# A decoder layer's expert gathers: the ring of 14 parts split into two circles of seven

## The chip, the cores and the metric

One core of a Trainium2 chip runs the whole layer in one launch. The metric is the device time of that core in microseconds (us), median over runs.

## What is computed

One decoder layer on 512 tokens of width 1024, in float32. A mixing sub-layer (stick-breaking attention with 8 heads and a gated MLP, side by side) comes first, then the PEER sub-layer, then a gated per-layer embedding; each ends in a LayerNorm over `alpha*x + f(x)`. The change lies in the PEER sub-layer. For every token and each of 8 heads, product keys choose 16 of 16384 experts. An expert is a row `u` and a row `v` of 1024 floats each:

```python
def block(args):                      # 128 tokens
    xb, idb, gb = args
    ue = jnp.take(u_tab, idb, axis=0)
    h = jnp.einsum('thkd,td->thk', ue, xb)
    act = gb * jax.nn.gelu(h, approximate=False)
    ve = jnp.take(v_tab, idb, axis=0)
    return jnp.einsum('thk,thkd->td', act, ve)
```

So 512 * 8 * 16 pairs of rows, 8 KB each, 537 MB, are fetched from HBM by index.

## The kernel before

The 512 tokens are four tiles of 128, one token to a partition. A *unit* is one tile with one head; 32 units stand in a fixed order (`UNITS`), and each has 16 *rows*. Row n = 16u + c is one expert for each of the 128 tokens: one indirect DMA, issued by POOL (GpSimd) at L691, takes 128 descriptors of 8 KB from the table `uv`, which holds each expert's u and v one behind the other. Its destination is 2 of the 14 parts of `ring` (L283), a part being 1024 floats on every partition: u in the first part, v in the next.

What happens to a row, engine by engine:

- POOL's `gather_unit` (L697) waits until the two parts are free and issues the gather, in the order of n.
- DVE's `dots` (L1906) waits for the landing and multiplies u with the token's vector and sums (L1914), which counts `dots_done` up; u is then no longer needed.
- ACT's `activate_rows` (L1521) takes two rows at a time: Gelu of the sums (L1526), times the gate (L1529), and the v part scaled in place by it (L1536).
- PE's `combine` (L1256) adds the scaled v part to the unit's sum in PSUM by eight transposing matmuls (L1269) and counts `slot_free` up; v is then no longer needed.

DVE ranks the next unit's keys between dots, and all of DVE, ACT and PE also do the mixing sub-layer of later tiles and the end of earlier ones between the rows, at steps written out by hand (`background`, one step for every two rows). SP loads weights by plain DMAs, which run on the same 16 DMA engines.

The ring's arithmetic: row n has its u at part `(8 + 11n) % 14` and its v in the part after it. Row n+5's v then falls on row n's u, and row n+9's u on row n's v. So `U_LIFE` is 5 and `V_LIFE` is 9: before the gather of row n, POOL waits for `slot_free` of row n-9 (L713), and then for `dots_done` of row n-5 (L718). Where a row's u falls on the last part its v falls on part 0, and it is *torn*: two gathers of 4 KB descriptors (L716 and L720). The first goes out ahead of the wait for `dots_done`.

```python
if torn(n):
    gather(u_row(u, c), u, c, 0, rows_in[c % LANDINGS])
if n >= U_LIFE and not (u == NU - 1 and c >= HOMED):
    pool.wait_ge(dots_done, n - U_LIFE + 1)
```

Eight landing semaphores (`LANDINGS`) go round with n. Of the last unit, rows from `HOMED` (13) on have homes of their own outside the ring, rows from `LATE` (11) on come with their v cut in half or left out, and seven small gathers fetch the rest at the end (L728 to L731). In the first unit the ring still holds weights of the first tile: the output projection's (parts 0 to 7), later scratch (8 and 9), the gating projection's (10 to 12, free in two steps, `gv_halves`), and a LayerNorm gain (13).

Of the kernel before, what the change touches and what calls it, by code (L numbers as in the profile page):

```python
# [24 lines left out]
PH, TOPK, NKEY = 8, 16, 128  # L25
# [6 lines left out]
MASKED = -float(2 ** 30)  # L32
SEED = 1597463007.0

U_LIFE, V_LIFE = 5, 9
PARTS = U_LIFE + V_LIFE
PART_STEP = 11
assert PART_STEP * U_LIFE % PARTS == PARTS - 1
FIRST_PART = 8
LANDINGS = 8  # L40
GRP = 2
OUT_PIECES = ((0, 512), (512, 832), (832, 1024))
# [6 lines left out]
HOMED = TOPK - 3  # L49
# [11 lines left out]
NU = len(UNITS)  # L61
# [17 lines left out]
assert RUN_END[NR - 1 - RUN_TILE[::-1].index(1)] == 21 and RUN_END[NR - 1 - RUN_TILE[::-1].index(2)] == 26  # L79


def part_of(n):

    return (FIRST_PART + PART_STEP * n) % PARTS


def torn(n):

    return n < (NU - 1) * TOPK + HOMED and part_of(n) == PARTS - 1


def landed(n):

    return sum(32 if torn(m) else 16 for m in range(n % LANDINGS, n + 1, LANDINGS))
# [124 lines left out]
def build(nc, a, out):  # L219
    ctx = ExitStack()  # L220
    with ctx:
# [3 lines left out]
        def sem(name):  # L225
            return ctx.enter_context(nc.semaphore(name))
# [71 lines left out]
        def row_home(u, c):  # L298
            return (v_flat, wq_a, wq_r)[c - HOMED]

        def u_row(u, c):

            if u == NU - 1 and c >= HOMED:
                return row_home(u, c)[:, 0:D]
            part = part_of(u * TOPK + c)
            return ring[:, part * D:(part + 1) * D]

        def v_row(u, c):

            if u == NU - 1 and c >= HOMED:  # L310
                return row_home(u, c)[:, D:2 * D]
            part = (part_of(u * TOPK + c) + 1) % PARTS
            return ring[:, part * D:(part + 1) * D]

        def whole_row(u, c):

            if u == NU - 1 and c >= HOMED:
                return row_home(u, c)
            part = part_of(u * TOPK + c)
            return ring[:, part * D:(part + 2) * D]  # L320

        late_sum = v_row(NU - 1, LATE)[:, HALF:D]
        y_1 = u_row(NU - 1, LATE)[:, 0:HALF]


# [165 lines left out]
        dots_done = sem("dots_done")  # L491
# [171 lines left out]
        @block.gpsimd  # L663
        def _(pool):
            nc.gpsimd.memset(ident[:, :], 0.0).then_inc(const_ready, 1)
            nc.gpsimd.memset(neg_tri[:, :], -1.0).then_inc(const_ready, 1)
            nc.gpsimd.memset(neg_one[:, :], -1.0).then_inc(const_ready, 1)
            nc.gpsimd.memset(neg_mask[:, :], MASKED).then_inc(const_ready, 1)
            nc.gpsimd.memset(ones[:, :], 1.0).then_inc(const_ready, 1)
            nc.gpsimd.iota(iota16[:, :], pattern=[[1, TOPK]], base=0, channel_multiplier=0,  # L670
                           allow_small_or_imprecise_dtypes=True).then_inc(const_ready, 1)
            pool.wait_ge(const_ready, 6)
            nc.gpsimd.affine_select(out=ident[:, :], in_=ident[:, :], compare_op=ALU.not_equal, fill=1.0,
                                    base=0, pattern=[[-1, P]], channel_multiplier=1).then_inc(const_ready, 1)
            nc.gpsimd.affine_select(out=neg_tri[:, :], in_=neg_tri[:, :], compare_op=ALU.is_ge, fill=0.0,
                                    base=0, pattern=[[-1, P]], channel_multiplier=1).then_inc(const_ready, 1)
            nc.gpsimd.affine_select(out=neg_mask[:, :], in_=neg_mask[:, :], compare_op=ALU.is_ge, fill=0.0,
                                    base=0, pattern=[[-1, P]], channel_multiplier=1).then_inc(const_ready, 1)
            pool.wait_ge(ws_in, 16)
            nc.gpsimd.affine_select(out=wsT, in_=wsT, compare_op=ALU.is_ge, fill=0.0, base=0,  # L680
                                    pattern=[[0, G], [1, P]], channel_multiplier=-1).then_inc(ws_masked, 1)


            for buf, ready, done in ((l_0, l_ready, l_masked), (e_0, a_ready, a_masked)):
                pool.wait_ge(ready, 1)
                blk = buf.rearrange("p i (h n) -> p (i h) n", n=P)
                nc.gpsimd.affine_select(out=blk, in_=blk, compare_op=ALU.is_gt, fill=0.0, base=0,
                                        pattern=[[0, AH], [1, P]], channel_multiplier=-1).then_inc(done, 1)

            def gather(dst, u, c, first, signal):  # L690
                nc.gpsimd.indirect_dma_start(  # L691
                    out=dst, out_offset=None, in_=a["uv"][:, :],
                    in_offset=bass.IndirectOffsetOnAxis(ap=ids[:, u % 4, c:c + 1], axis=0),
                    element_offset=first,
                ).then_inc(signal, 16)

            def gather_unit(u):  # L697
                if u:
                    pool.wait_ge(ids_ready, u + 3)
                for c in range(TOPK):  # L700
                    n = u * TOPK + c
                    if u == 0 and c in (0, 1, TOPK // 2):
                        pool.wait_ge(ids_ready, (0, 1, TOPK // 2).index(c) + 1)
                    if u == 0 and c == 0:
                        pool.wait_ge(score_done, 1)
                    if u == 0 and c == 4:
                        pool.wait_ge(gv_halves, 1)
                    if u == 0 and c == 8:
                        pool.wait_ge(gv_halves, 2)
                    if u == NU - 1 and c >= HOMED:  # L710
                        pool.wait_ge(q_done, NU)
                    elif n >= V_LIFE:
                        pool.wait_ge(slot_free, n - V_LIFE + 1)  # L713
                    end = PART if u == NU - 1 and c >= LATE else 2 * D
# [5 lines that stand above are left out]
                        gather(v_row(u, c)[:, 0:end - D], u, c, D, rows_in[c % LANDINGS])  # L720
                    elif u == NU - 1 and c >= TOPK - 2:
                        gather(u_row(u, c), u, c, 0, rows_in[c % LANDINGS])
                    else:
                        gather(whole_row(u, c)[:, 0:end], u, c, 0, rows_in[c % LANDINGS])

            for u in range(NU):
                gather_unit(u)
            for c in range(TOPK - 2, TOPK):  # L728
                gather(v_row(NU - 1, c)[:, 0:HALF], NU - 1, c, D, values_in[c - TOPK + 2])
            for c in range(LATE, TOPK):  # L730
                gather(v_row(NU - 1, c)[:, HALF:D], NU - 1, c, PART, late_in[c - LATE])  # L731
# [1493 lines left out]
```

## Time and profile before

| | us |
|---|---|
| median of 3 runs | 1422.82 (1420.91 to 1423.07) |
| the profiled execution | 1421.98 |
| its span, first to last instruction | 1420.3 |
| PE busy / DVE / ACT / POOL | 1130.9 / 1078.1 / 938.8 / 625.0 |
| POOL's gathers, 556 instructions | 619.9 |
| DVE's dots, 512 instructions | 623.1 (467.7 and 155.4) |

The profile is of one execution. "Busy" is the time in which an engine ran an instruction; waiting, branching and issuing by SP are not counted. A DMA share is the mean busy share of 16 DMA engines; packets that overlap on an engine can bring it above 1. The granted TensorE clock was 0.896 of full speed over the span.

### The profile page before, as it was taken

Reading aid. Unit: us, or ns where it says so; the run is one execution under the profiler, and the core shown is the slowest. Engines: PE = TensorE matmul, PEld = TensorE weight load, DVE = VectorE, ACT = ScalarE, POOL = GpSimd, SP = SyncE. Lnnn points to the kernel's source line nnn. Section 1 sums busy time; section 2 is a strip of 40 time slices with the busy share of each in tenths; the row PEclk is TensorE's granted clock in tenths of the full one; section 3 lists DMA queues with packets and bytes.
Section 4 is the critical chain, followed back from the end, with each engine's and each line's share of the span. In section 5 each row is a group of like instructions: output and inputs, shape, how many; then the busy total and the mean of one; then the engine's idle time right before and its main releaser. Section 6 shows DMA issues by size and latency. Waiting matters only on the chain.

```text
span 1420.3 us, 19525 instructions
## 1 busy us (share of the span) xinstructions
PE 1130.9 (80%) x6884; PEld 890.8 (63%) x6884; DVE 1078.1 (76%) x2602; ACT 938.8 (66%) x1617; POOL 625.0 (44%) x572
## 2 busy tenths in 40 slices
PE   9999999998789877696756987877667866776566
PEld 4567777676677776666656566765555655555455
DVE  1488877778778887678766668988887788878857
ACT  2245778679877988766645666667666766667563
POOL 1044444344444554444433434444444555444451
PEclk9999999999889999998777988898789988888968
DMA  9899999999999999999999999999999999999994
GB/s 351 311 383 409 422 425 425 426 425 425 402 426 419 424 423 425 425 424 417 431 422 425 426 426 406 426 425 426 426 426 413 404 423 426 426 425 426 425 400 170
DMA packets 94476, 581.98 MB, mean 410 GB/s; under 512 B 10237, under 2 KB 15781, under 8 KB 31914
## 3 DMA queue, kind: packets, MB, share of 16 engines
q0 software_dynamic: 79552, 536.91, 90.5%
q1 hardware_dynamic: 14826, 43.83, 8.0%
q8 instruction: 54, 0.88, 0.2%
q14 instruction: 44, 0.36, 0.1%
HBM read 578.60 MB, written 2.10 MB: 409 GB/s over the span
## 4 chain that ended last, share of the span: by engine, by line
DMA 40%; PE 30%; DVE 15%; ACT 8%; issue 6%; POOL 2%; SPq 0%; DVEq 0%; POOLq 0%; ACTq 0%
DMA arena<-in_uv,ids 39%; PE ps L1269 11%; DVE arena L1914 8%; ACT arena L1536 3%; PE ps L1082 3%; PE ps L948 3%; POOL arena L691 2%; PE ps L1159 2%; PE ps L740 2%; ACT actv L1529 1%; PE ps L757 1%; PE ps L896 1%; PE ps L824 1%; PE ps L821 1%; ACT L1576 1%
## 5 line engine op out<-in xcount | busy, mean ns | idle before, releaser
L691 POOL DMA_INDIRECT arena<-in_uv,ids x556 | 619.9, 1115 | 734.5 <-DVE hid L1914 338.0
L1269 PE MATMUL ps<-ident,arena 128*128 128x128 f32 x4076 | 608.9, 308 | 273.0 <-ACT arena L1536 271.2
L1269 PEld LDWEIGHTS ps<-ident,arena 128*128 128x128 f32 x4076 | 533.3, 159 | 364.6 <-ACT arena L1536 321.4
L1914 DVE CUSTOM_DVE_ANT_1 arena<-arena 128x1024 f32<-128x1024 f32 x384 | 467.7, 1224 | 187.2 <-DMA arena<-in_uv,ids 183.8
L1536 ACT ACTIVATE arena<-arena,actv 128x1024 f32<-128x1024 f32 x511 | 554.2, 1131 | 0.3 <-ACT actv L1529 0.2
L1526 ACT ACTIVATE gel<-hid 128x2 f32<-128x2 f32 (+1 forms) x257 | 52.0, 202 | 356.0 <-DVE hid L1914 353.2
L1914 DVE CUSTOM_DVE_ANT_0 arena<-arena 128x1024 f32<-128x1024 f32 x128 | 155.4, 1223 | 61.1 <-DMA arena<-in_uv,ids 58.5
L1529 ACT ACTIVATE actv<-gel,gates 128x1 f32<-128x1 f32 x511 | 122.9, 287 | 8.4
L948 PE MATMUL ps<-arena 128*128 128x128 f32 x992 | 120.3, 281 | 0.0
L948 PEld LDWEIGHTS ps<-arena 128*128 128x128 f32 x992 | 118.2, 199 | 0.0
L1082 PE MATMUL ps<-arena 128*128 128x384 f32 x192 | 65.9, 486 | 0.0
L1159 PE MATMUL ps<-arena 128*128 128x512 f32 (+2 forms) x160 | 60.2, 524 | 0.0
L1576 ACT ACT_TABLE_LOAD x45 | 57.7, 1283 | 0.8
L1584 ACT ACT_TABLE_LOAD x45 | 57.7, 1283 | 0.8
L1082 PEld LDWEIGHTS ps<-arena 128*128 128x128 f32 x192 | 34.6, 190 | 19.1
L896 PE MATMUL ps<-arena 128*128 128x512 f32 x96 | 43.9, 600 | 0.7 <-DVE arena L1924 0.4
L1159 PEld LDWEIGHTS ps<-arena 128*128 128x128 f32 x160 | 29.9, 201 | 20.9 <-issue 18.5
L1914 DVE DVE_READ_ACCUMULATOR2_ANT hid<- 128x1 f32 x512 | 41.9, 82 | 0.0
L747 PE MATMUL ps<-arena 128*128 128x512 f32 x64 | 29.4, 599 | 1.3 <-ACT arena L1427 0.7
L896 PEld LDWEIGHTS ps<-arena 128*128 128x128 f32 x96 | 17.7, 194 | 18.9 <-issue 17.5
L740 PE MATMUL ps<-arena 128*128 128x512 f32 x64 | 28.9, 594 | 0.0
L1783 DVE TENSOR_TENSOR cands<-cands,topf 128x512 f32<-128x512 f32 x31 | 21.4, 691 | 1.1
(269 smaller groups left out, 1018.1 us busy)
## 6 DMA issues: line engine op xcount, KB each, us to landing
arena<-in_wq SPq DMA_DIRECT2D x9, 1024.0 KB, 10.2
arena<-in_uv,ids POOLq DMA_INDIRECT x556, 3.8
arena<-in_w_out SPq DMA_DIRECT2D x2, 2048.0 KB, 11.3
arena<-in_w_gate SPq DMA_DIRECT2D x1, 4096.0 KB, 17.2
arena<-in_w_out SPq DMA_DIRECT2D x3, 1024.0 KB, 13.1
arena<-in_w_k SPq DMA_DIRECT2D x4, 512.0 KB, 7.9
arena<-in_w_q SPq DMA_DIRECT2D x2, 1024.0 KB, 10.2
arena<-in_w_v SPq DMA_DIRECT2D x2, 1024.0 KB, 10.2
```

What stands on the lines that cost most here:

```text
L691: nc.gpsimd.indirect_dma_start(out=dst, out_offset=None, in_=a["uv"][:, :], in_offset=bass.IndirectOffsetOnAxis(ap=ids[:, u % 4, c:c + 1], ...
L740: i = mm(ps[:, bank, :], xt(k), w[:, k * AW:(k + 1) * AW], start=(k == 0), stop=(k == KD - 1), skip_group_check=True)
L896: i = mm(ps[:, bank, :], src[:, c, :], w[:, c, j * HALF:(j + 1) * HALF], start=(c == 0), stop=(c == WB - 1))
L948: i = mm(ps[:, 7, half * P:(half + 1) * P], wq[b][k][:, half * P:(half + 1) * P], x1T[t][:, k, :], start=(k == 0), stop=(k == KD - 1))
L1082: i = mm(ps[:, piece_bank(p), 0:REST], w[:, b * D + k * P:b * D + (k + 1) * P], xT[:, k, :], start=(k == 0), stop=(k == KD - 1), skip_grou ...
L1159: m = mm(ps[:, bank, place:place + c1 - c0], acc[t][:, k * P:(k + 1) * P], w_gate[:, k, c0:c1], start=(k == 0 and place == 0), stop=(k == ...
L1269: i = mm(ps[:, run_bank(r) + k // 4, (k % 4) * P:(k % 4 + 1) * P], v_row(u, c)[:, k * P:(k + 1) * P], ident[:, :], is_transpose=True, star ...
L1529: fn(actv[:, i, c:c + 1], gel[:, i, c:c + 1], ACT.Copy, scale=gates[:, i, c:c + 1])\
L1536: fn(r, r, ACT.Copy, scale=actv[:, i, c:c + 1]).then_inc(scaled, 1)
L1576: act.preload_act_table_set("natural_log_exp_and_others")
L1584: act.preload_act_table_set("gelu_and_others")
L1914: v.tensor_tensor_reduce(out=r, in0=r, in1=x1[t], scale=1.0, scalar=0.0, op0=ALU.mult, op1=ALU.add, accum_out=hid[:, i, c:c + 1]).then_inc ...
```

## The change

The 14 parts become two circles of seven, one for rows of even n and one for odd n. In its circle a row's u is at `(first + 2 * (n // 2)) % 7` and its v in the next part of that circle. Row n+6's v then falls on row n's u, and row n+8's u on row n's v: `U_LIFE` is 6 and `V_LIFE` 8. A row whose u falls on the last part of its circle is torn, one row in seven. Two waits of the first unit move (from row 4 to 5 and from row 8 to 7), and the last unit's homed rows wait for `dots_done` of row n-8, the one that used their landing semaphore before.

```diff
--- before.py
+++ after.py
@@ -32,11 +32,12 @@
 MASKED = -float(2 ** 30)
 SEED = 1597463007.0
 
-U_LIFE, V_LIFE = 5, 9
+U_LIFE, V_LIFE = 6, 8
 PARTS = U_LIFE + V_LIFE
-PART_STEP = 11
-assert PART_STEP * U_LIFE % PARTS == PARTS - 1
-FIRST_PART = 8
+CIRCLE = PARTS // 2
+PART_STEP = 2
+assert PART_STEP * U_LIFE // 2 % CIRCLE == CIRCLE - 1
+FIRST_PART = (0, 6)
 LANDINGS = 8
 GRP = 2
 OUT_PIECES = ((0, 512), (512, 832), (832, 1024))
@@ -79,14 +80,24 @@
 assert RUN_END[NR - 1 - RUN_TILE[::-1].index(1)] == 21 and RUN_END[NR - 1 - RUN_TILE[::-1].index(2)] == 26
 
 
-def part_of(n):
-
-    return (FIRST_PART + PART_STEP * n) % PARTS
+def place_of(n):
+
+    return (FIRST_PART[n % 2] + PART_STEP * (n // 2)) % CIRCLE
+
+
+def u_part(n):
+
+    return n % 2 * CIRCLE + place_of(n)
+
+
+def v_part(n):
+
+    return n % 2 * CIRCLE + (place_of(n) + 1) % CIRCLE
 
 
 def torn(n):
 
-    return n < (NU - 1) * TOPK + HOMED and part_of(n) == PARTS - 1
+    return n < (NU - 1) * TOPK + HOMED and place_of(n) == CIRCLE - 1
 
 
 def landed(n):
@@ -302,21 +313,21 @@
 
             if u == NU - 1 and c >= HOMED:
                 return row_home(u, c)[:, 0:D]
-            part = part_of(u * TOPK + c)
+            part = u_part(u * TOPK + c)
             return ring[:, part * D:(part + 1) * D]
 
         def v_row(u, c):
 
             if u == NU - 1 and c >= HOMED:
                 return row_home(u, c)[:, D:2 * D]
-            part = (part_of(u * TOPK + c) + 1) % PARTS
+            part = v_part(u * TOPK + c)
             return ring[:, part * D:(part + 1) * D]
 
         def whole_row(u, c):
 
             if u == NU - 1 and c >= HOMED:
                 return row_home(u, c)
-            part = part_of(u * TOPK + c)
+            part = u_part(u * TOPK + c)
             return ring[:, part * D:(part + 2) * D]
 
         late_sum = v_row(NU - 1, LATE)[:, HALF:D]
@@ -703,12 +714,13 @@
                         pool.wait_ge(ids_ready, (0, 1, TOPK // 2).index(c) + 1)
                     if u == 0 and c == 0:
                         pool.wait_ge(score_done, 1)
-                    if u == 0 and c == 4:
+                    if u == 0 and c == 5:
                         pool.wait_ge(gv_halves, 1)
-                    if u == 0 and c == 8:
+                    if u == 0 and c == 7:
                         pool.wait_ge(gv_halves, 2)
                     if u == NU - 1 and c >= HOMED:
                         pool.wait_ge(q_done, NU)
+                        pool.wait_ge(dots_done, n - LANDINGS + 1)
                     elif n >= V_LIFE:
                         pool.wait_ge(slot_free, n - V_LIFE + 1)
                     end = PART if u == NU - 1 and c >= LATE else 2 * D
```

## Rows read from the trace of the kernel before

**Rows 1.** The page: busy times, DMA share in 40 slices, the gathers' queue, their issues.
```profile
PE 1130.9 (80%) x6884; PEld 890.8 (63%) x6884; DVE 1078.1 (76%) x2602; ACT 938.8 (66%) x1617; POOL 625.0 (44%) x572
...
DMA  9899999999999999999999999999999999999994
...
q0 software_dynamic: 79552, 536.91, 90.5%
...
arena<-in_uv,ids POOLq DMA_INDIRECT x556, 3.8
```

**Rows 2.** Stretches: length, busy PE, PEld, DVE, ACT, POOL (count), clock, DMA share, GB/s.
```profile
160.00:180.00 20.00, 20.00 (x133) 15.65 (x128) 14.67 (x38) 12.51 (x22) 7.25 (x8) 1.00 1.02 426
...
340.00:360.00 20.00, 13.29 (x114) 11.90 (x112) 18.29 (x49) 18.82 (x28) 8.47 (x9) 0.89 0.97 399
...
860.00:880.00 20.00, 15.61 (x116) 14.20 (x115) 17.76 (x28) 14.06 (x27) 9.78 (x8) 0.91 0.96 392
1080.00:1100.00 20.00, 10.41 (x73) 8.83 (x71) 17.45 (x48) 11.27 (x21) 10.52 (x9) 0.91 1.00 404
1100.00:1120.00 20.00, 20.00 (x114) 14.85 (x113) 14.78 (x26) 13.73 (x26) 10.08 (x8) 0.92 0.98 387
1200.00:1220.00 20.00, 10.88 (x67) 9.31 (x66) 17.17 (x48) 11.50 (x21) 10.62 (x9) 0.81 1.01 425
1340.00:1360.00 20.00, 13.82 (x66) 10.11 (x65) 16.68 (x38) 14.02 (x24) 10.54 (x8) 0.77 0.95 385
```

**Rows 3.** Order of time: start, length, what, idle before and releaser; POOL's holes.
```profile
356.23 1.16 POOL L691 DMA_INDIRECT arena<-in_uv,ids  x1 [5.79 <-issue]
...
1348.58 1.22 DVE L1914 CUSTOM_DVE_ANT_1 arena<-arena 128x1024 f32<-128x1024 f32 x1
...
1353.14 2.01 POOL L691 DMA_INDIRECT arena<-in_uv,ids  x1 [4.64 <-issue]
```

**Rows 4.** Order of time near the end of the gathers, the same columns.
```profile
1373.11 1.23 DVE L1914 CUSTOM_DVE_ANT_1 arena<-arena 128x1024 f32<-128x1024 f32 x1 [1.21 <-DMA arena<-in_uv,ids]
...
1373.75 3.67 PE L1269 MATMUL ps<-ident,arena 128*128 128x128 f32 x16 [1.75 <-ACT arena L1536]
...
1375.54 1.23 DVE L1914 CUSTOM_DVE_ANT_1 arena<-arena 128x1024 f32<-128x1024 f32 x1 [1.20 <-DMA arena<-in_uv,ids]
...
1377.56 0.94 POOL L691 DMA_INDIRECT arena<-in_uv,ids  x1 [1.15 <-PE ps L1269]
...
1381.59 0.94 POOL L691 DMA_INDIRECT arena<-in_uv,ids  x1 [0.30 <-issue]
...
1386.63 1.23 DVE L1914 CUSTOM_DVE_ANT_1 arena<-arena 128x1024 f32<-128x1024 f32 x1 [0.61 <-DMA arena<-in_uv,ids]
```

**Rows 5.** Waits of POOL: us in total, times, longest.
```profile
POOL arena L691 <- DVE hid L1914: 338.0, 186, 6.4
POOL arena L691 <- PE ps L1269: 271.2, 158, 5.4
```

**Rows 6.** DMA queues (packets, MB, share) in 704:718 (two), 1200:1300 and 5:30 us.
```profile
q1 hardware_dynamic: 113, 3.64, 60.2%
q0 software_dynamic: 331, 2.36, 40.1%
...
q0 software_dynamic: 6265, 42.48, 101.0%
...
q1 hardware_dynamic: 5999, 9.33, 103.0%
```

**Rows 7.** Order of time: gathers and combines early on, while PE is full.
```profile
170.40 0.98 POOL L691 DMA_INDIRECT arena<-in_uv,ids  x1 [3.37 <-PE ps L1269]
...
446.23 1.03 POOL L691 DMA_INDIRECT arena<-in_uv,ids  x1 [0.30 <-issue]
...
447.32 1.91 PE L1269 MATMUL ps<-ident,arena 128*128 128x128 f32 x16
```

**Rows 8.** Order of time: row 4's gather in the first unit.
```profile
82.33 0.93 POOL L691 DMA_INDIRECT arena<-in_uv,ids  x1 [1.55 <-PE ps L747]
```

## Prediction

> **What bounds the kernel now.** I read the page first. The gathers' queue holds 90.5% of all 16 DMA engines' time, the DMA digit is 9 in every slice but the second and the last, and PE, the busiest engine, is busy for 80% [rows 1]. So bytes on the move set the pace. The table of stretches sharpens it: where nothing disturbs the stream it moves 425 or 426 GB/s at a DMA share of 1.01 or 1.02, whether PE is busy 20 us of 20 or 11 [rows 2]. A row is 1.05 MB, so it takes 2.47 us there. A change to the ring can then act in three ways only: it fills stretches that lie below that rate, it opens new ones, or it makes the same bytes dearer.
>
> Second, the stretches below it. 340 to 360, 860 to 880, 1100 to 1120 and 1340 to 1360 us stand at shares of 0.97, 0.96, 0.98 and 0.95, with 385 to 399 GB/s [rows 2]. The order of time on POOL has a hole in each of them, and one more between: five gathers before which POOL sat idle for about 5 us, the first at 356.23 and the last at 1353.14 [rows 3]. The last can be followed. Counted back from the last dot product, the one of row 492 ended at 1349.80 (1348.58 and 1.22) and freed the u part for row 497's gather; that gather started 3.34 us later [rows 3]. At row 508 the same step, from the end of row 503's dot (1375.54 and 1.23) to the gather at 1377.56, took 0.79 [rows 4]. So five times POOL itself is some 2.55 us late after its wait is over. What holds it there the trace doesn't tell.
>
> Third, which wait holds a gather. The view of waits gives DVE's dot 338.0 us and PE's combine 271.2 [rows 5], but it names the semaphore that moved last, not the count that was needed. In order of time, row 508's gather came 0.79 us after the dot of row 503, while the combine that it needs, of row 499, was over before PE began rows 500 and 501 at 1373.75 [rows 4]. Followed through the trace like this, the dot of row n-5 comes after the combine of row n-9 for all but some 17 rows: the u part's life is the gate, the v part's has slack. From that gather to its own dot at 1386.63 lie 9 us [rows 4]: four rows are in flight.
>
> **The change, part by part.** The sum is made against the profiled execution's own time, 1421.98 us (span 1420.3), 0.8 below the median of the runs.
>
> *One row more ahead on the u side, one fewer on the v side.* Row n's gather now waits for the dot of n-6 and the combine of n-8. At row 508 that is the dot of 502, over at 1374.34, and the combine of 500, the first eight of the sixteen matmuls that began at 1373.75 and took 3.67, so about 1375.6 [rows 4]. PE becomes the later of the two, and the release moves from 1376.77 to 1375.6: 1.2 us earlier, not the full 2.47 that it would be behind a quick combine. In an undisturbed stretch this is worth nothing, since the DMA engines have work for 9 us anyway. In the holes it covers a gather that is 2.55 us late. What they cost now: against a share of 1.01 the four stretches lack 0.04, 0.05, 0.03 and 0.06 of 20 us, 0.8 + 1.0 + 0.6 + 1.2 = 3.6 us; by bytes against 425 GB/s they lack 1.2 + 1.6 + 1.8 + 1.9 = 6.5 us [rows 2]. I take 3.6, since the share counts idle engines alone while smaller packets lower GB/s too, and I take all of it back, since 1.2 us of cover is more than a hole loses on the mean. The ends are 0 and 6.5.
>
> *A torn row in every seven.* Counted by the two formulas, 73 rows are torn where 37 were: 36 more gathers, 592 for 556. Each makes 128 packets of 8 KB into 256 of 4 KB and adds 16 small ones of its own, 144 packets. What a packet costs beside its bytes comes from two stretches: 444 packets with 6.00 MB took 100.3% of 16 engines for 14 us, 224.7 us, and 6265 with 42.48 MB took 101.0% for 100 us, 1616 us [rows 6]. Solved, a packet costs 8.1 ns and a MB 36.9 us. 144 packets on 16 engines are 0.073 us a row, 2.6 us for 36. The upper end comes from a stretch of small packets, 5999 with 9.33 MB at 103.0% for 25 us, 412 us [rows 6]: with the same 1616 us that is 12.4 ns and 4.0 us. The lower end is 0: shares over 1 say that packets overlap, and the overhead may be what overlaps. I take 2.6, from a stretch of the big packets that the stream is made of. POOL issues 36 times more, at 0.94 and a gap of 0.30 as at 1381.59 [rows 4], 45 us in all. It is busy 44% [rows 1] and waits for the ring before nearly every gather, so that hides; uncovered, a torn row would leave 1.24 us later. The first gather of a torn row goes before the wait for the dot, which only deepens the queue.
>
> *PE as the gate early on.* At 160 to 180 us PE is busy 20 us of 20 [rows 2], and combines run late there: a gather at 170.40 already had POOL idle for 3.37 us behind one [rows 7]. The dearest place that I find is at 446.23. That gather (row 142) would now wait for the first half of the sixteen matmuls of 447.32, until some 448.3, and start near 449.1, 2.9 us later than it did [rows 7]. A gather needs 3.8 us from issue to landing (that median is of the quarter-sized ones at the end [rows 1]) and a whole row some 1.8 more, so 454.7. Row 141 landed at about 452.1, ahead of its dot, and the stream wants the next 2.47 later, at 454.6: it just misses. I take 0.4 for all such places, with ends of 0 and 3.5 (four such places, each short by 0.9, what a gather's issue can grow by: it took 0.94 at best and 2.01 at 1353.14 [rows 3]).
>
> *Start and end, at nothing.* The waits for the projections of the gate move from rows 4 and 8 to rows 5 and 7. Gathers run there already and the third slice (71 to 106 us) is at 9 [rows 1], so the stream is full; without that cover it would be the 1.55 us that POOL waited for PE at 82.33 [rows 8]. The three homed rows get a wait for the dot of row n-8: for row 511 that is row 503's, over at 1376.77, while its gather came at 1381.59 behind others that POOL issues one after another [rows 4]. Only POOL's last seven gathers stand behind it, and none is held.
>
> The sum: -3.6 + 2.6 + 0.4 = -0.6, and the time 1421.4 us.
>
> **The rivals.** *Faster: the holes cost what the bytes say.* Then 6.5 come back: -6.5 + 2.6 + 0.4 = -3.5, 1418.5. For it: 385 GB/s is 9% below the rate where the share is 6% below, and the holes lie in the low stretches. Against it: 1080 to 1100 is low as well, 404 GB/s, and has no hole [rows 2].
>
> *Slower: PE's combine gates the stream.* With v parts kept for eight rows, a gather can't leave before PE is done with row n-8. It decides where a combine ends over some 14 us after its row landed: seven rows of 2.47 in flight, less the 3.8 that a gather needs [rows 1]. If it stands at the holes too, nothing comes back there, and the near misses cost their end: 2.6 + 3.5 = 6.1, 1428.1. For it: PE full in the first 300 us. Against it: at row 508 the combine still releases earlier than the dot did.
>
> *The longer life does nothing.* If POOL's delay starts anew at whatever row it waits for and eats the cover, the holes stay and the packets are paid: +2.6 + 0.4, 1425.0.
>
> *Every added gather holds up the stream for its fixed time.* If the queue ran dry for the 3.8 us from issue to landing [rows 1], 36 would cost 137 us, 1559. Against it: 100 us move 42.48 MB, forty rows, with some 9 us of flight each [rows 6, 4], so these times overlap. The Trainium skill (DMA: Bandwidth & Descriptors, Anatomy of one DMA) speaks against splitting: some 2.0 us fixed for each such DMA, beside its bytes at 436 GB/s; paid one after another that would be an estimated 72 us for 36. The 37 torn rows of the kernel before show no gap of that kind.
>
> **How the numbers follow.** 0.2% of this kernel, 2.8 us, is about what a measurement can tell from no change: faster is below 1420.0, slower above 1425.7. The forecast has 0.51. The faster rival has 0.26, and with it the case that the packets cost nothing, 1418.8 with the forecast's other terms. PE as the gate has 0.16, the useless longer life 0.06 (a third of it over the line, with packets at their upper end), the fixed time 0.01. So faster 0.26, same 0.55, slower 0.19. The range runs from 1417.5, past the faster cases, to 1426.5, past the useless life and into PE's gate.
>
> **What would show it.** Right: 592 gathers; the stretches around POOL's late gathers at a share of 1.01; packets under 8 KB in the middle of the span nearly doubled and its rate 1 GB/s lower; POOL's waits shifted from the dot to the combine. Wrong: new stretches below 1.00 before 460 us with PE full (PE's gate), holes as deep as now (the useless life), or an unchanged rate with the stream over 3 us earlier (free packets, or dearer holes).

## The result and the profile after

The changed kernel takes 1424.12 us, median of 22 runs (1421.4 to 1428.38), beside 1422.71 for 22 runs of the kernel before (1419.86 to 1424.46). The ratio is 1.0013 (1.0007 to 1.0019): 1.8 us slower, between 1.0 and 2.7; by the medians alone 1.4. The forecast was 1421.4, 0.6 us faster than the profiled execution of before. The time lies inside the range given and within the 0.2% called no change, but the sign is the other one. The profiled execution took 1423.77 us (span 1422.1, granted clock 0.903 of full speed).

The page of the changed kernel, the lines that answer to [rows 1], with the group of POOL's gathers from its fifth part:

```profile
PE 1126.8 (79%) x6884; PEld 881.7 (62%) x6884; DVE 1080.1 (76%) x2602; ACT 939.0 (66%) x1617; POOL 678.2 (48%) x608
...
DMA  9899999999999999999999999999999999999993
...
q0 software_dynamic: 84800, 536.91, 90.5%
...
L702 POOL DMA_INDIRECT arena<-in_uv,ids x592 | 673.2, 1137 | 681.0 <-PE ps L1281 393.4
...
arena<-in_uv,ids POOLq DMA_INDIRECT x592, 11.4
```

592 gathers, as counted. POOL's largest wait is for PE, and a gather now takes a median of 11.4 us from issue to landing. (The 3.8 of the kernel before covers only the few gathers of which every landing mark was recorded; the same ring in v8_late, below, shows 9.9.) (Lines 702, 1281 and 1926 of the changed kernel are 691, 1269 and 1914 of the kernel before.) The view of waits of the changed kernel, POOL's two largest, beside [rows 5]:

```profile
POOL arena L702 <- PE ps L1281: 393.4, 212, 5.6
POOL arena L702 <- DVE hid L1926: 147.2, 66, 6.4
```

The dot's share fell from 338.0 to 147.2 us and the combine's rose from 271.2 to 393.4: the gate moved to PE, as forecast. Followed row by row, the combine of row n-8 comes after the dot of row n-6 for 336 of the 500 rows from 9 to 508. The table of stretches of the changed kernel (columns as in [rows 2]):

```profile
160.00:180.00 20.00, 20.00 (x125) 15.55 (x124) 14.21 (x36) 11.94 (x22) 8.51 (x8) 1.00 1.00 392
340.00:360.00 20.00, 13.32 (x120) 12.20 (x119) 18.09 (x51) 19.09 (x28) 11.74 (x11) 0.94 1.01 419
440.00:460.00 20.00, 17.95 (x127) 14.65 (x126) 17.62 (x37) 19.72 (x31) 9.91 (x8) 1.00 0.93 369
860.00:880.00 20.00, 16.71 (x104) 14.57 (x103) 18.63 (x38) 14.29 (x25) 7.95 (x8) 0.74 1.01 426
1100.00:1120.00 20.00, 18.73 (x108) 14.53 (x109) 15.73 (x32) 14.61 (x27) 8.96 (x10) 0.91 1.01 426
1200.00:1220.00 20.00, 10.56 (x64) 8.98 (x64) 17.24 (x43) 11.52 (x23) 10.33 (x10) 0.83 1.02 425
...
1260.00:1280.00 20.00, 17.16 (x87) 11.91 (x87) 15.54 (x32) 14.28 (x27) 10.35 (x9) 0.91 1.00 399
...
1340.00:1360.00 20.00, 12.84 (x69) 10.24 (x70) 17.70 (x43) 14.38 (x25) 10.55 (x10) 0.84 1.02 426
```

The four low stretches of before, at 0.95 to 0.98 and 385 to 399 GB/s [rows 2], stand at 1.01 or 1.02. New low ones came: 160 to 180 us (392 GB/s where [rows 2] has 426), 440 to 460 (369), and 1260 to 1280 (399), around a gather that POOL, itself late, issued at 1277.86; its row and the two behind it still landed 2.45 to 2.48 us apart, on time. One stretch of the kernel before, not shown until now:

```profile
440.00:460.00 20.00, 19.70 (x135) 15.76 (x135) 17.47 (x35) 19.71 (x31) 10.36 (x10) 1.00 1.01 418
```

So the changed kernel gains where the holes were and loses early on. POOL's late gathers themselves now come at other rows (99, 191, 283, 375 and 467), so that the four stretches are full doesn't yet show that the longer life covers a late gather; a_u5 below bears on that. The order of time of the changed kernel shows the first of the new places on POOL and PE, then the gather of row 142 that the prediction picked, then the last dot (columns as in [rows 3]):

```profile
160.92 1.92 POOL L702 DMA_INDIRECT arena<-in_uv,ids  x1 [3.12 <-PE ps L1281]
...
164.93 3.60 PE L752 MATMUL ps<-arena 128*128 128x512 f32 x8
168.37 1.04 PE L1281 MATMUL ps<-ident,arena 128*128 128x128 f32 x8
...
169.68 0.94 POOL L702 DMA_INDIRECT arena<-in_uv,ids  x1 [3.37 <-PE ps L1281]
...
174.45 0.98 POOL L702 DMA_INDIRECT arena<-in_uv,ids  x1 [2.52 <-PE ps L1281]
...
178.78 0.94 POOL L702 DMA_INDIRECT arena<-in_uv,ids  x1 [2.11 <-PE ps L1281]
...
447.77 1.91 PE L1281 MATMUL ps<-ident,arena 128*128 128x128 f32 x16
...
449.08 1.85 POOL L702 DMA_INDIRECT arena<-in_uv,ids  x1 [4.97 <-PE ps L1281]
...
1392.61 1.23 DVE L1926 CUSTOM_DVE_ANT_1 arena<-arena 128x1024 f32<-128x1024 f32 x1
```

At 169.68 goes row 36's gather. It waited 3.37 us for the combine of row 28, the eight matmuls at 168.37; PE had a v projection of 3.60 us (L752) ahead of them. It landed at 175.81, 2.44 behind row 35 and so on time, 6.1 us after its issue. Row 37, issued next, landed 2.93 behind it, and row 38, whose gather at 174.45 had waited again, 3.44 behind that, where 2.47 keep the stream full: some 1.5 us lost in three rows.

### The profile page after: what moved, and what is told of

It reads as the page before. It is cut to its first block, busy times and chain, and to the rows that moved or that the text cites. A ratio compares the mean times of both kernels' runs of the same rounds, so it can differ in the third digit from the quotient of the medians.

```text
span 1422.1 us, 19535 instructions
## 1 busy us (share of the span) xinstructions
PE 1126.8 (79%) x6884; PEld 881.7 (62%) x6884; DVE 1080.1 (76%) x2602; ACT 939.0 (66%) x1617; POOL 678.2 (48%) x608
## 4 chain that ended last, share of the span: by engine, by line
DMA 40%; PE 30%; DVE 12%; ACT 8%; issue 6%; POOL 4%; SPq 0%; POOLq 0%; DVEq 0%; ACTq 0%
DMA arena<-in_uv,ids 39%; PE ps L1281 11%; DVE arena L1926 7%; ACT arena L1548 4%; POOL arena L702 4%; PE ps L1094 3%; PE ps L960 3%; PE ps L1171 2%; PE ps L759 2%; ACT actv L1541 1%; PE ps L769 1%; PE ps L752 1%; ACT L1596 1%; ACT L1588 1%; PE ps L833 1%
## 5 line engine op out<-in xcount | busy, mean ns | idle before, releaser
L702 POOL DMA_INDIRECT arena<-in_uv,ids x592 | 673.2, 1137 | 681.0 <-PE ps L1281 393.4
L1281 PEld LDWEIGHTS ps<-ident,arena 128*128 128x128 f32 x4076 | 527.5, 158 | 372.6 <-ACT arena L1548 330.8
L1588 ACT ACT_TABLE_LOAD x45 | 57.7, 1283 | 0.8
L1596 ACT ACT_TABLE_LOAD x45 | 57.7, 1283 | 0.8
L752 PE MATMUL ps<-arena 128*128 128x512 f32 x64 | 28.9, 594 | 0.0
## 6 DMA issues: line engine op xcount, KB each, us to landing
arena<-in_uv,ids POOLq DMA_INDIRECT x592, 11.4
```

The costliest lines, as they stand in the source:

```text
L702: nc.gpsimd.indirect_dma_start(out=dst, out_offset=None, in_=a["uv"][:, :], in_offset=bass.IndirectOffsetOnAxis(ap=ids[:, u % 4, c:c + 1], ...
L1281: i = mm(ps[:, run_bank(r) + k // 4, (k % 4) * P:(k % 4 + 1) * P], v_row(u, c)[:, k * P:(k + 1) * P], ident[:, :], is_transpose=True, star ...
L1588: act.preload_act_table_set("natural_log_exp_and_others")
L1596: act.preload_act_table_set("gelu_and_others")
```

## The experiments

Every kernel is compared with 29 to 35 runs of the kernel before on the same chip (median 1421.47 for v8_only, a_u5 and the two split kernels, 1421.8 for the three light kernels and shift3, 1421.58 for the rest); differences in us come from the ratio, and the interval behind a ratio is at 95%. "v8" below means the wait for the combine of row n-8 where the kernel before waits for that of n-9, and nothing else.

**The combine's wait alone** (v8_only): the old ring, the wait one row tighter.

```diff
-                    elif n >= V_LIFE:
-                        pool.wait_ge(slot_free, n - V_LIFE + 1)
+                    elif n >= V_LIFE - 1:
+                        pool.wait_ge(slot_free, n - V_LIFE + 2)
```

> The kernel before, where the gather of row n also waits for the combine of row n-8 (it needs only n-9). So the new gate of the change alone: no longer life for u, no more torn rows. Theory A: +1 to +3 us, from new short gaps of the stream at 165 to 180 us and 445 to 460 us, where PE is full, and holes unchanged. Rival B (all of the change's loss beyond the holes is this gate): +5 to +6 us. If the gate is harmless: 0.

1425.27 us (1421.25 to 1431.32, 12 runs), ratio 1.0029 (1.0014 to 1.0043): +4.1 us, between 2.0 and 6.1. Its stretches show the same two places:

```profile
160.00:180.00 20.00, 20.00 (x122) 15.33 (x121) 13.63 (x34) 11.83 (x22) 8.05 (x8) 1.00 0.99 400
440.00:460.00 20.00, 19.80 (x128) 15.03 (x127) 17.49 (x37) 19.72 (x32) 10.54 (x9) 1.00 0.99 387
```

The shorter v life alone costs more than the whole change does, and ten times the 0.4 that I took for it.

**Where it costs** (v8_early, v8_late): the same wait for rows under 200 only, and from 200 on only.

```diff
-                    elif n >= V_LIFE:
-                        pool.wait_ge(slot_free, n - V_LIFE + 1)
+                    elif n >= V_LIFE - 1:
+                        pool.wait_ge(slot_free, n - V_LIFE + 1 + (n < 200))
```

(v8_late has `n >= 200` and leaves the `elif` as it was.)

> The kernel before, where the gathers of rows 8 to 199 also wait for the combine of row n-8, and the rest for n-9 as before. Theory A (the gate bites while PE does the later tiles' projections and attention between the combines, in the first 550 us): the whole of what the gate cost for all rows, +3 to +4 us. Rival (the gate costs a little at every row): 200/512 of it, +1.6 us.

> The same wait for row n-8, for rows from 200 on alone. Theory A: 0, within 0.1%. Rival: 312/512 of what the gate costs for all rows, +2.5 us.

v8_early: 1424.83 (11 runs), 1.0023 (1.0012 to 1.0035), +3.3 us. v8_late: 1421.95 (12 runs), 1.0000 (0.9992 to 1.0009), nothing that shows. The first stretch, of v8_early and then of v8_late:

```profile
160.00:180.00 20.00, 20.00 (x137) 15.65 (x134) 14.62 (x37) 13.71 (x25) 8.30 (x8) 1.00 1.00 401
```

```profile
160.00:180.00 20.00, 20.00 (x131) 15.65 (x128) 15.05 (x38) 13.17 (x25) 7.56 (x9) 1.00 1.01 425
```

The price lies in the first 200 rows, before some 600 us. In the other 312 no price of the tighter wait shows (-1.1 to 1.3 us).

**One row tighter still** (v7_only): the wait for the combine of n-7, in the old ring.

```diff
-                    elif n >= V_LIFE:
-                        pool.wait_ge(slot_free, n - V_LIFE + 1)
+                    elif n >= V_LIFE - 2:
+                        pool.wait_ge(slot_free, n - V_LIFE + 3)
```

> The kernel before, where every gather also waits for the combine of row n-7: two rows tighter than its ring needs. The dose. In the profile of before a combine ends 7.4 us after its row landed at the median, 10.9 at 90 in 100 and up to 13.9; seven rows less the lead leave some 11 us. Theory A: many rows of the first 550 us and some later ones bind, +10 to +25 us, mostly before 550 us. If the gate's cost doesn't come from late combines: twice the cost of one row, +8 us, evenly spread.

1452.97 (1448.09 to 1463.25, 4 runs), 1.0206 (1.0185 to 1.0228): +29 us, more than the 10 to 25 expected. Two of its stretches, from a profile of the slowest of the four runs:

```profile
160.00:180.00 20.00, 20.00 (x124) 15.47 (x123) 12.38 (x35) 12.49 (x22) 8.00 (x8) 1.00 0.89 336
...
1200.00:1220.00 20.00, 11.71 (x66) 10.25 (x67) 15.79 (x40) 11.06 (x20) 9.74 (x9) 0.70 1.01 425
```

Full rate late, far from it early. The prices for a v life of nine, eight and seven rows are 0, 4 and 29: the lag of the combine has a tail that a life of nine just covers and eight just doesn't.

**Is it PE's load?** (light, light_v8, light_after): three kernels with less work on PE. Half of the contraction is left out of the later tiles' k, q, v and gate projections and of the output projection, so these compute something else; the gathers, dots and combines are all there. `light` does this to the kernel before, `light_v8` to v8_only, `light_after` to the changed kernel.

```diff
-                    i = project_tok(piece_bank(p), w_v, x_cols(b), 4 * half, 4 * half + 4)
+                    for k in range(4 * half, 4 * half + 2):
...
-                    for k in range(4 * half, 4 * half + 4):
+                    for k in range(4 * half, 4 * half + 2):
...
-                for c in range(WB):
+                for c in range(WB // 2):
```

> The kernel before with PE relieved: the projections of the later tiles' k, q, v and gate over half of their depth (four of eight matmuls each half piece becomes two), and the output projection of the later tiles over two of four blocks. It leaves that part of the computation out; bytes, DVE, ACT and POOL are as before. It is the base for the next two. The stream bounds, so both theories expect it within 0.2% of before.

> The same relieved kernel, with every gather also waiting for the combine of row n-8. The gate alone cost +0.29% (0.14 to 0.43) at full PE work. Theory A (the gate costs because PE's other work makes the early combines late): under a third of that against the relieved kernel, 0 to +1.4 us, and the stretches 160:180 and 440:460 at a DMA share of 1.00 or more. Rival (the wait itself costs, whatever PE does, as one more wait of POOL before every gather or later issues all along): +4 us again.

> The changed kernel relieved in the same way. Theory A: with the gate harmless the change shows its gain, 0 to 3 us faster than the relieved kernel before. Rival: +2 us as at full PE work.

light: 1422.01, 1.0003 (0.9994 to 1.0012). light_v8: 1425.46, 1.0026 (1.0014 to 1.0038), which is 3.45 over light. light_after: 1422.86, 1.0002 (0.9989 to 1.0015), level with light. By these counts the relief did not take the price of the wait away. The stretches say where it did and where it didn't. Of light_v8:

```profile
160.00:180.00 20.00, 17.36 (x109) 12.78 (x107) 14.77 (x38) 12.39 (x24) 7.97 (x8) 1.00 1.02 426
440.00:460.00 20.00, 16.16 (x116) 13.45 (x117) 17.32 (x35) 19.45 (x30) 10.15 (x10) 1.00 1.00 410
460.00:560.00 100.00, 78.52 (x607) 71.13 (x606) 79.77 (x195) 85.16 (x136) 49.38 (x43) 0.90 1.01 416
```

and of light:

```profile
440.00:460.00 20.00, 17.71 (x114) 14.05 (x113) 17.59 (x37) 19.72 (x32) 10.58 (x9) 0.83 1.01 424
460.00:560.00 100.00, 79.90 (x624) 72.76 (x623) 81.53 (x200) 86.05 (x139) 50.51 (x44) 0.90 1.01 424
```

At 160 to 180 us, where PE fell from 20.00 busy to 17.36, the stream is back at 426. Between 440 and 560 the relief took little off PE in the long stretch (80.24 in v8_only, 78.52 here), and the rate stays below light's: 410 against 424 and 416 against 424, (14/424)*20 + (8/424)*100 = 2.5 us. The order of time of light_after at the first place (its combine is line 1283):

```profile
170.98 2.13 PE L1283 MATMUL ps<-ident,arena 128*128 128x128 f32 x16 [0.57 <-ACT arena L1550]
```

The combine there waits for ACT, not behind a projection. So early on it is PE's queue that makes the combine late. What makes it late between 440 and 560 us the relief doesn't tell: ACT is busy 19.45 of 20 us there, and the output projection waits for DVE as well; neither was tested.

**The landings.** Each gather leaves sixteen landing marks in the trace, and a row can be used at its last one. How much later the last mark came than in the kernel before (for the two light kernels: than in light), us, median of seven rows, one execution of each, worked out from the marks (some 7% of them are missing in the kernel before, none in the changed one):

```
row   changed  v8_only  v8_early  v8_late  a_u5  |  light_v8  light_after
 31     -0.8     -0.8      1.4      0.5     0.1  |    -1.1       -1.9
 60      2.1      2.2      4.2      0.3     2.1  |    -1.8       -1.8
139      0.4      1.4      4.5     -0.4     1.5  |    -1.1       -1.1
194      3.3      4.0      6.8     -0.4     3.5  |     1.3        1.9
230      1.5      3.4      5.8     -0.7     1.9  |     0.6       -0.3
395      2.2      3.6      5.9     -0.4     3.3  |     1.3        1.2
506      1.7      3.6      5.9      0.8     4.0  |     1.9        1.0
```

Down a column, two steps stand in the changed kernel, v8_only and v8_early alike: 2.8 to 3.0 us between rows 31 and 60, and 2.3 to 2.9 between 139 and 194. v8_late has neither. With PE relieved the first step is gone, the second isn't. In the changed kernel 1.5 of the first is rows 37 and 38 as above; another 1.5 is row 47, whose first mark came on time and whose last one came 3.7 later than a full stream would bring it behind row 46 (in the kernel before, row 48's came 2.2 late); no wait of POOL explains that. What makes the second step stays open.

**The packets** (p1_split36, p2_split255): more torn rows in the old ring, in which any row can be fetched as two gathers. 36 more, and 255 more.

```diff
-    return n < (NU - 1) * TOPK + HOMED and part_of(n) == PARTS - 1
+    return n < (NU - 1) * TOPK + HOMED and (part_of(n) == PARTS - 1 or n % 2 == 0)
```

(p1_split36 has `n % PARTS == 10` in place of `n % 2 == 0`.)

> The kernel before with its own ring (u for 5 rows, v for 9) and 36 more torn rows (every n that leaves 10 by 14), so 73 as in the changed kernel; nothing else. Theory A (packets paid, holes won back, combines as a new gate): 36 times 0.073 us, +2.6 us, up to 4.0; about 1.002 of before. Rival B (packets are free, the whole difference is PE's combine as the gate): 0, within 0.1%. The holes on POOL come once every 105 gathers in both profiles, so they should come every 98 - 6 = 92 rows here and stay holes of the stream.

> The kernel before with every even row of the ring torn as well, 255 more gathers than before. The packets' price enlarged. Theory A: 255 times 0.073 us, +18.6 us (0.05 to 0.111 a row: 13 to 28). Rival B: 0 to 3 us. A third reading, that each added gather costs the stream some fixed time of the order of 1 us, gives over 100 us. POOL then issues 1.57 gathers a row, 1.95 us of 2.47, so it should still keep up; holes on POOL come every 105 gathers, so 8 instead of 5, some 3 more at 0.8 us.

p1_split36: 1421.9 (12 runs), 0.9999 (0.9989 to 1.0009). p2_split255: 1431.71 (6 runs), 1.0064 (1.0051 to 1.0077), +9.1 us, below the 13 to 28 expected. The issues on p2_split255's page, and its gathers' queue in 1200 to 1300 us:

```profile
arena<-in_uv,ids POOLq DMA_INDIRECT x811, 8.8
...
q0 software_dynamic: 9111, 42.08, 101.7%
```

255 splits at 9.1 us are 0.036 us each (0.028 to 0.043), half of the 0.073 that I worked out from two stretches. (The 9.1 holds two more late gathers of POOL as well, seven for five, so 0.036 is if anything too much.) For 36, at the same price each, that is 1.3 us (1.0 to 1.5). p1_split36 alone can't tell 1.3 from nothing, and its added gathers also shift the rows at which POOL is late.

**Shifting POOL's late gathers** (shift3, shift11): three and eleven rows more are torn early on, which moves the late gathers and does hardly anything else.

```diff
-    return n < (NU - 1) * TOPK + HOMED and part_of(n) == PARTS - 1
+    return n < (NU - 1) * TOPK + HOMED and (part_of(n) == PARTS - 1 or n in (10, 24, 38))
```

(shift11 has `n in range(10, 76, 6)`.)

> The kernel before with three more torn rows, 10, 24 and 38, and nothing else. POOL is late once in 105 gathers, so its five holes move three rows forward, to rows 102, 200, 298, 396 and 494, where by the trace of before DVE has just been quick: the next landings lie 8.3 to 8.6 us behind the release, against 6.6 to 8.2 at rows 105 to 497. Theory A (what a hole costs is decided by the row that it falls on; much of the change's gain came from moving the holes, not from the longer life): 2 to 4 us faster than before. Rival (a hole costs the same wherever it falls while u lives five rows): 0.

> The kernel before with eleven more torn rows, every sixth from 10 to 70: POOL's holes move eleven rows forward, to rows 94, 192, 290, 388 and 486, where the next landings lie 8.5 to 11.6 us behind the release by the trace of before. Theory A (a hole costs by where it falls): 1 to 3 us faster than before, like the kernel with three more torn rows, of which the stream's gaps were half of those before. Rival (where they fall doesn't matter): +0.4 us for the packets.

shift3: 1420.97 (11 runs), 0.9993 (0.9984 to 1.0002). shift11: 1421.81 (11 runs), 0.9997 (0.9988 to 1.0005). Neither is clear of no difference; what a shift alone could bring is 1 us or so. The late gathers moved as meant: rows 102, 200, 298, 396 and 494 in shift3, 95, 194, 293, 392 and 491 in shift11. In p1_split36 they stand at rows 99, 191, 283, 374 and 467, none of which lands between 860 and 880 us, and still that stretch of p1_split36 is low:

```profile
860.00:880.00 20.00, 15.75 (x93) 13.43 (x92) 17.57 (x28) 12.93 (x25) 10.06 (x9) 0.74 0.99 390
```

**The longer u life taken back** (a_u5): the changed kernel, whose gather of row n waits for the dot of n-5 again. Two circles, torn rows and the wait for PE stay.

```diff
-                    if n >= U_LIFE and not (u == NU - 1 and c >= HOMED):
-                        pool.wait_ge(dots_done, n - U_LIFE + 1)
+                    if n >= U_LIFE - 1 and not (u == NU - 1 and c >= HOMED):
+                        pool.wait_ge(dots_done, n - U_LIFE + 2)
```

> The changed kernel, where the gather of row n also waits for the dot of row n-5, as before the change (it needs only n-6). So the longer life of u is taken back; packets and PE's gate stay. Theory A: slower than the changed kernel by what the holes cost, 3.6 to 6.5 us, so some +5 to +8 us over before, and gaps of the stream at POOL's late gathers again. If the longer life did nothing: equal to the changed kernel, +1.4 us over before.

1426.28 (1423.05 to 1428.35, 12 runs), 1.0027 (1.0016 to 1.0038), +3.8 us, less than the 5 to 8 expected. The changed kernel's ratio is 0.0014 lower, so the longer life is worth 2.0 us; with both intervals, 0.2 to 3.8. Both are late at the gather of row 375. The stretch there, of a_u5 and then of the changed kernel:

```profile
1040.00:1060.00 20.00, 12.06 (x72) 10.18 (x70) 15.76 (x40) 11.06 (x20) 11.18 (x10) 0.77 0.98 392
```

```profile
1040.00:1060.00 20.00, 13.73 (x74) 11.73 (x72) 15.85 (x42) 11.39 (x23) 11.86 (x10) 0.67 1.02 428
```

The same late gather opens a hole with five rows ahead and none with six. By the marks, rows 375 and 376 of a_u5 land 2.81 and 2.80 us behind the row before and row 467, at the next late gather, 3.17; in the changed kernel these are 2.44, 2.53 and 2.48. The four stretches that were low in the kernel before don't tell the two apart. Of a_u5:

```profile
340.00:360.00 20.00, 14.46 (x118) 13.39 (x116) 16.98 (x52) 17.81 (x28) 11.80 (x10) 0.90 1.01 423
860.00:880.00 20.00, 16.02 (x112) 14.42 (x112) 18.63 (x36) 13.91 (x25) 8.36 (x10) 0.88 1.01 423
1100.00:1120.00 20.00, 18.41 (x116) 13.82 (x115) 15.63 (x33) 14.29 (x25) 11.61 (x10) 0.99 1.02 424
1340.00:1360.00 20.00, 11.69 (x67) 9.00 (x66) 17.43 (x45) 14.02 (x24) 12.08 (x11) 0.84 1.01 425
```

They are full with u kept for five rows as well: the 36 added gathers bring POOL's late ones to other rows.

No kernel here clearly beats both. A ring that keeps u five rows and v nine up to row 200, and six and eight after it, should by these numbers have the gain without the price; it wasn't tried, since the two layouts would have to hand over in the middle of the stream.

## Why the prediction was wrong

**The step that failed is "PE as the gate early on".** It was given 0.4 us, with ends of 0 and 3.5. Alone it measured 4.1 (2.0 to 6.1), 3.3 of it in the first 200 rows and nothing that shows behind them. Two things in the step were wrong. First, I looked for the dearest single gather and named row 142's. In the changed kernel that gather came at 449.08, forecast near 449.1, and its row landed 2.46 us behind row 141: it did not miss at all. (In v8_only and v8_early rows 142 and 143 together lost 1.0 and 0.7 us against v8_late: this place can cost, but it is a part.) The other one in the same group I passed over: [rows 7] shows POOL idle for 3.37 us behind a combine at 170.40, and I did not follow the rows behind it. In the changed kernel one gather after another waits for PE there, the queue runs down, and 1.5 us are lost by row 38. Row 47 and the second step of the table hold the rest, and how they come about no run shows. Second, the lead that a gather needs: I took 3.8 + 1.8 = 5.6 us from issue to landing, the first term from the quarter-sized gathers of the end. Row 36 took 6.1 and row 142 6.4 (449.08 to 455.50), each with the row before it still landing. Of the prediction's own signs of being wrong one came true: a new stretch below 1.00 before 460 us, at 0.93 from 440 on, though its rows landed on time.

**The packets** were right in kind and, if 36 cost by the piece what 255 did, half in size: 1.3 us for the forecast 2.6. That lies between the bounds given; that packets overlap would fit it, but no run shows that this is the reason.

**The holes.** All four stretches came back to a share of 1.01, as forecast, but not by what I forecast: in a_u5, without the longer life, they are as full. The added gathers move POOL's late ones to other rows, which the prediction did not reckon with. Where the late ones now fall, rows 375 and 467 show the cover at work. It is worth 2.0 us (0.2 to 3.8) where 3.6 was forecast. "A hole in each of them" was too simple: 860 to 880 us is low in p1_split36 without one.

**The sum.** Packets and moved holes come together, so I add runs. p1_split36 has both, at -0.1 (-1.6 to 1.3); with 4.1 for the gate that is 4.0, and a_u5, which has the three together, measured 3.8. Less 2.0 for the longer life, 4.0 gives +2.0; measured +1.8 (1.0 to 2.7). Packets and holes, forecast at -3.6 + 2.6 = -1.0, came out at -0.1 - 2.0 = -2.1, within their intervals somewhat better. The gate came out 3.7 worse, and it alone turned the sign.

**The rivals.** "PE's combine gates the stream" had the mechanism that decided and, at its end, nearly the price; its claim that nothing would come back at the holes was wrong, and so was its time, 1428.1. The faster rival took 6.5 for the holes; no run gave back that much. "The longer life does nothing" falls by row 375. The fixed time for each gather falls by p2_split255: 255 more gathers cost 9.1 us, while 255 times the 3.8 us from issue to landing would be 969. The Trainium skill (DMA: Bandwidth & Descriptors, Anatomy of one DMA) puts some 2.0 us of fixed cost on each such DMA, an estimated 510 us for 255; the run shows under 2% of that; here the next gather is in flight all the while, as the 8.8 us from issue to landing on p2_split255's page tell for rows of 2.47.

**Start and end** cost nothing that shows: the landings are within 0.8 us of before at row 31, and the last seven gathers run back to back.

## What to carry to other kernels

When a ring trades a row of life between two consumers, price the shorter life by the tail of that consumer's lag in its busiest stretch, over several rows in a row, not by one gather or by the stage in which the profile looks tight on the mean. A wait can be tightened alone in the old kernel before anything is rebuilt, and for one part of the loop at a time; here one line told the price, and a second its place. A price too small to measure can be multiplied: 255 splits told what 36 couldn't.

## What the runs showed that was not expected

**The DMA engines drift apart, and bytes are not rows.** The first and the last landing mark of a gather lay 1.3 us apart in the kernel before around row 500 (2.3 in v8_late, of which no mark is missing), and 4.8 in the changed one; at row 440 it was 2.6 and 5.8. In a_u5, with the same torn rows and u kept for five, it was 2.9 and 3.6. So with one row more ahead the engines that are ahead run further. The Trainium skill (DMA: Bandwidth & Descriptors, Why a DMA increments its semaphore by 16 and not by 1) says that each mark is one engine's, and that only all sixteen mean that the data are there; the Trainium skill (the same page, Latency and other measured facts) has two engines, 7 and 15, as usually slower in traces, with a best guess at the cause. Which engine a mark is from can't be read here. So a stretch's GB/s counts bytes that no one can use yet. The dip of 369 at 440 to 460 us is mostly that: row 141's marks spread from 448.45 to 453.03, row 142's from 454.83 to 455.50. The fast engines lost their lead, and the row was on time. The end shows the same. The gathers' queue in 1380 to 1400 us, of the kernel before and then of the changed one:

```profile
q0 software_dynamic: 1455, 5.88, 73.6%
```

```profile
q0 software_dynamic: 1313, 5.42, 69.7%
```

At 1380 us the changed kernel had 0.46 MB less to fetch, 1.1 us at 425 GB/s, and yet its last dot began at 1392.61, where the kernel before began its own at 1391.02:

```profile
1391.02 1.22 DVE L1914 CUSTOM_DVE_ANT_1 arena<-arena 128x1024 f32<-128x1024 f32 x1
```

Sizing a hole by the mean share of sixteen engines, as I did, counts idle time of engines that were ahead as well.

**POOL is late once in about 105 gathers**, whatever row it is: every 105th gather in the kernel before (the 114th, 219th, 324th, 429th and 534th), 105 or 106 apart in the changed one, 106 in shift11 and some 102 in p2_split255. It starts some 3.3 us after its wait is over where 0.79 is usual. Counting gathers places it better than rows or time do; its cause stays open.
